# A feed-forward by seven block products: another sequence of the products, second buffers for two block sums, and other places for the first activation slabs

## The chip, the cores and the metric

One core of a Trainium2 chip runs one launch that computes two transformer blocks on a sequence of 1024 tokens. The metric is the device time of that core in microseconds (us). Three timed runs of the kernel before took 2768.13, 2770.41 and 2771.04 us, so the median is 2770.41 us.

## The reference, cut to what matters

Everything is float32. The change touches only the feed-forward of the first block and the hand-over into it and out of it. `conv_glu_ffn` multiplies the normed input h (1024 tokens x 1024 features) with `ffn_w_up` (1024 x 5632), runs a causal depthwise convolution of three taps with a bias over tokens, multiplies silu(gate) by value, and multiplies the product (1024 x 2816) with `ffn_w_down`:

```python
x = x + conv_glu_ffn(rmsnorm(x, ffn_norm_g[l]), ffn_w_up[l], ffn_conv_w[l],
                     ffn_conv_b[l], ffn_w_down[l])
```

## The kernel before, in words

**Numbers.** Every float32 matrix product is made of three products of rounded parts (`dot3`, L980): high weight by high activation, high by low, low by high. A high part is a rounding copy, on ScalarE for the weights of this stage (`high_...`, L2079 to L2111) and for activations (`t_high_part`, `b2_high_part`, `block_high`, `diff_high`); a low part is the value less its high part, on GpSimd for the weights (`pair_part`, L882) and on VectorE for activations (`t_low`, `b1_low`, `b2_low`).

**Up product.** The 5632 output features are 22 pairs (one gate tile and one value tile of 128 features). A pair is a 2 x 2 block product: the weights' blocks are A11, A12 (gate; first and second half of the contraction) and A21, A22 (value); the activations' blocks are B11, B21 (tokens 0 to 511) and B12, B22 (tokens 512 to 1023). Seven block products of twelve matmuls each (four 128-slices of contraction, three parts) replace eight, with the block sums S1 = A21+A22, S2 = S1-A11, S3 = A21-A11, S4 = A12-S2 made by GpSimd for every pair, and T1, T2, T3, T4 of the activations made once by VectorE (`t_diff`). The products, in the order before, are A11 B11, S1 T1, S3 T3, S2 T2, A12 B21, S4 B22, A22 T4. They go into four half banks a, c, d, b of `gemm0` and `gemm1`; A12 B21 is added onto a, S4 B22 onto c, A22 T4 onto d, and a copy of what stood there must be out first: `snapshot(p, 0)` of a, `snapshot(p, 1)` of c (ScalarE, L2162), and VectorE's sum of d with that copy of c (L2978). VectorE's further sums (`up_sums`, `up_gate`, `up_value`) give gate and value, scaled per token by WIDE_FF; then come the convolution taps (ScalarE `tap2` for the last, VectorE `tap` for the others), Silu (ScalarE `gate`), their product (VectorE `product`), and its store to `act_spill` in HBM.

**Where things lie.** h_hi/h_lo hold B11 and T1 in slices 0 to 3, B21 and B22 in slices 4 to 7. T2, T3, T4 have buffers of their own. S2, S3 and S4 have one buffer each, so GpSimd waits for the product of the pair before (`prod_mm`) that read them.

**Entry.** The norm's factor of a token (1/rms) is not applied to h; the sums of squares (`add_square`, VectorE) go through 16 thin matmuls (`token_sums`, L1138), a root (ScalarE, L2160), a reciprocal (VectorE, L2968), a spread over partitions (`spread`, L1144, before product 7 of pair 0) and a copy into WIDE_FF (ScalarE, L2223). Each is queued at one place of its engine's written order. The last tile of the residual x (m = 7) is added by VectorE at L2938, after the last matmul of the layer before.

**Down product.** Eleven steps per half of the output features, each of 48 matmuls, read `act_spill` back in slabs of two tiles. The slabs go through a ring of three buffers, those of T3, T2 and T4 (`RING`, `ring_load`, `ring_high_part`, `ring_low`). A step waits for its split weights (`w_split`; GpSimd, `split_slot`) and for both low halves of its slab (`ring_ready`); step 0 also for VectorE's last reads of the banks.

**What sets the order.** Nothing is planned at run time: each engine's instructions are written out in one order (SP's for loads and stores), each waits on counting semaphores, and an engine stands still at the first wait that is not met.

Of the kernel before, what the change touches and what calls it, by code (L numbers as in the profile page):

```python
# [8 lines left out]
F32 = mybir.dt.float32  # L9
F32R = mybir.dt.float32r  # L10
I32 = mybir.dt.int32
ALU = mybir.AluOpType
# [109 lines left out]
RING = [(i, i % N_RING) for i in range(FF_STEPS)] + [(i, N_RING - 1 - i % N_RING) for i in range(FF_STEPS - 2)]  # L122
# [71 lines left out]
def build(nc, w_stream, x_t, mem_t, positions, vecs, rows, small_w, pool_w, consts, x_spill, c_rows, out):  # L194
    ctx = ExitStack()
    with ctx:
# [31 lines left out]
        hhi = sb("h_hi", [P, KT, S], F32R)  # L228
        hlo = sb("h_lo", [P, KT, S], F32R)
        with nc.sbuf_tensor("pair_ex_f", [P, KT, P], F32) as pair_ex_f, nc.sbuf_tensor("v_gate1_r", [P, KT, P], F32R) as v_gate1_r, \  # L230
                nc.sbuf_tensor("v_val1_r", [P, KT, P], F32R) as v_val1_r:
            pass
        with nc.sbuf_tensor("pair_ex", [P, KT, P], F32R) as pair_ex, nc.sbuf_tensor("v_gate1", [P, KT, P], F32) as v_gate1, \
                nc.sbuf_tensor("v_val1", [P, KT, P], F32) as v_val1, nc.sbuf_tensor("taps", [P, 4, S], F32) as taps:
# [36 lines left out]
        S2_V, S3_V, S4_V = pair_ex_f[:, LO, :], wlo_f0[:, LO, :], wlo_f1[:, LO, :]  # L271
        S2_R, S3_R, S4_R = pair_ex[:, LO, :], wlo[0][:, LO, :], wlo[1][:, LO, :]
# [8 lines left out]
        def lows(p):  # L281

            gate, val = r_pair[p % 2]
            return gate[:, LO, :], val[:, LO, :], S3_R, S2_R, gate[:, HI, :], S4_R, val[:, HI, :]
# [5 lines left out]
        ring_f = [flat4(t3_lo_f), flat4(t2_lo_f), flat4(t4_lo_f)]  # L290
        X = xres[:, :, :].rearrange("p k s -> p (k s)")
# [59 lines left out]
        T_ORDER = [(k, n) for k in range(2) for n in range(3)] + [(2, 0), (2, 1), (3, 0), (3, 1), (2, 2), (3, 2)]  # L351

        def t_at(k, n):

            return T_ORDER.index((k, n)) + 1
# [263 lines left out]
        def _(sp):  # L619
# [66 lines left out]
            ring_load(0)  # L686
            act_store(PAIRS - 2)
            ring_load(1)
            down_load(2)
            ring_load(2)  # L690
            down_load(3)
            act_store(PAIRS - 1)
            for e in range(4, len(DOWN)):
                if e == 4:
# [3040 lines left out]
```

## Time and profile before

| | us |
|---|---|
| median of three timed runs | 2770.41 |
| the profiled execution | 2770.92 |
| its span, first to last instruction | 2769.1 |
| PE busy in the span | 2711.5 |
| DVE, POOL, ACT busy in the span | 1433.2, 1121.4, 1051.2 |

PE is TensorE, DVE is VectorE, ACT is ScalarE, POOL is GpSimd, SP is the engine that issues most transfers. A time stamp is in us from the span's start. The up product of pair 0 begins at about 672 us, the down product at about 1121 us. A matmul's listed duration overlaps the next one's; the distance of two starts tells the pace. "Idle before" is the time an engine stood still ahead of an instruction, with what released it.

### The profile page before, as it was taken

The numbers are of one execution on the slowest core, as the hardware profiler recorded it, in microseconds if no ns is written. First come the engines' busy times: TensorE is split into PE (matmuls) and PEld (weight loads), VectorE is DVE, ScalarE is ACT, GpSimd is POOL, SyncE is SP. The second block draws the span as 40 slices with busy tenths as digits, with TensorE's granted clock in tenths as the row PEclk, the third lists the DMA queues.
The fourth block names the chain that finished last, engine by engine and source line by source line (L and its number), as shares of the span: only waits on it lengthen the run. The fifth ranks groups of instructions, "written<-read, shape, count | busy, mean of one in ns | idle before, by whom it ended". The sixth has DMA issues, their size and how long they took to land.

```text
span 2769.1 us, 34511 instructions
## 1 busy us (share of the span) xinstructions
PE 2711.5 (98%) x13574; PEld 2190.9 (79%) x13574; DVE 1433.2 (52%) x2014; ACT 1051.2 (38%) x1598; POOL 1121.4 (40%) x625
## 2 busy tenths in 40 slices
PE   8999999998999999999999999999998999999998
PEld 6888787777788888788878888888876777777776
DVE  7344643137656666422456666666545444444455
ACT  5322222334444444221245455454434333333342
POOL 4333453224676767434322222222345333333335
PEclk9999999999999999999999999999998999999999
DMA  4012231002122222554322222222222111111114
GB/s 152 31 46 74 102 100 53 31 28 102 69 83 77 85 76 84 198 175 138 114 87 72 56 64 72 64 71 64 57 99 86 41 39 38 38 38 39 38 52 163
DMA packets 111785, 214.21 MB, mean 77 GB/s; under 512 B 32032, under 2 KB 61888, under 8 KB 111504
## 3 DMA queue, kind: packets, MB, share of 16 engines
q1 hardware_dynamic: 104992, 190.02, 20.9%
q10 hardware_dynamic: 6192, 20.18, 2.0%
q8 instruction: 108, 1.77, 0.3%
q0 software_dynamic: 448, 1.88, 0.2%
q14 instruction: 45, 0.37, 0.0%
HBM read 177.38 MB, written 34.67 MB: 77 GB/s over the span
## 4 chain that ended last, share of the span: by engine, by line
PE 90%; DVE 5%; ACT 2%; issue 2%; DMA 1%; POOL 0%; SPq 0%; ACTq 0%; DVEq 0%; POOLq 0%
PE gemm L982 21%; PE gemm L983 21%; PE gemm L984 21%; PE small L1164 2%; PE small L1702 2%; PE small L1680 2%; PE small L984 1%; PE small L983 1%; PE small L982 1%; PE small L1690 1%; PE small L1552 1%; PE gemm L1105 1%; PE gemm L1109 1%; PE gemm L1108 1%; PE small L1277 1%
## 5 line engine op out<-in xcount | busy, mean ns | idle before, releaser
L982 PE MATMUL gemm<-h_hi,w_hi 128*128 128x512 f32 x2120 | 902.1, 426 | 21.5 <-DVE h_lo L2674 8.9
L983 PE MATMUL gemm<-h_lo,w_hi 128*128 128x512 f32 x2120 | 840.4, 396 | 0.0
L984 PE MATMUL gemm<-h_hi,w_lo 128*128 128x512 f32 x1944 | 769.7, 396 | 0.0
L796 POOL TENSOR_TENSOR w_hi<-w_raw,unit_col 128x1024 fp32r<-128x1024 f32 x134 | 264.4, 1973 | 1133.9 <-PE gemm L984 888.8
L982 PEld LDWEIGHTS gemm<-h_hi,w_hi 128*128 128x128 f32 x2120 | 401.6, 189 | 108.5 <-issue 13.3
L983 PEld LDWEIGHTS gemm<-h_lo,w_hi 128*128 128x128 f32 x2120 | 402.2, 190 | 79.3 <-issue 6.2
L984 PEld LDWEIGHTS gemm<-h_hi,w_lo 128*128 128x128 f32 x1944 | 366.3, 188 | 88.7
L805 POOL TENSOR_TENSOR w_lo<-w_raw,w_hi 128x1024 fp32r<-128x1024 f32 x118 | 305.6, 2590 | 13.8 <-DVE w_lo L2833 4.9
L943 POOL TENSOR_TENSOR w_hi<-w_raw,unit_col 128x1024 fp32r<-128x1024 f32 x32 | 60.7, 1896 | 324.6 <-PE gemm L984 324.6
L2503 ACT ACTIVATE xres<-xres,stat 128x128 f32<-128x128 f32 (+3 forms) x64 | 49.7, 777 | 206.0 <-DVE stat L3508 205.2
L3030 DVE TENSOR_TENSOR t_lo<-t_lo_f,t_hi 128x1024 fp32r<-128x1024 f32 x40 | 48.9, 1264 | 149.3 <-ACT t_hi L2205 149.3
L3012 DVE SCALAR_TENSOR_TENSOR small<-norm,vec,small 128x1024 f32<-128x1024 f32 x84 | 108.1, 1287 | 30.7 <-ACT small L2191 28.4
L3502 DVE SCALAR_TENSOR_TENSOR xres<-small,rstd_cols,xres 128x128 f32<-128x128 f32 x64 | 22.5, 351 | 175.0 <-PE small L1680 166.5
L982 PE MATMUL gemm<-t_hi,w_hi 128*128 128x512 f32 x264 | 105.3, 399 | 0.6 <-DVE norm L2993 0.3
L983 PE MATMUL gemm<-t_lo,w_hi 128*128 128x512 f32 x264 | 105.0, 398 | 0.0
L984 PE MATMUL gemm<-t_hi,w_lo 128*128 128x512 f32 x264 | 104.3, 395 | 0.0
L2205 ACT ACTIVATE t_hi<-t_lo_f 128x1024 fp32r<-128x1024 f32 x40 | 40.2, 1051 | 161.2 <-DMA t_lo_f<-act_spill 161.2
L2587 ACT ACTIVATE xres<-small 128x512 f32<-128x512 f32 (+2 forms) x96 | 47.1, 490 | 106.1 <-PE small L1690 105.4
L2191 ACT ACTIVATE small<-norm,vec 128x1024 f32<-128x1024 f32 x42 | 50.7, 1207 | 75.9 <-DVE norm L2993 74.1
L1702 PEld LDWEIGHTS small<-xres 128*128 128x128 f32 x576 | 74.1, 191 | 5.7
L945 POOL TENSOR_TENSOR w_lo<-w_raw,w_hi 128x1024 fp32r<-128x1024 f32 x32 | 76.5, 2392 | 2.5
L1702 PE MATMUL small<-xres 128*128 128x128 f32 x576 | 74.5, 274 | 0.0
(526 smaller groups left out, 5176.9 us busy)
## 6 DMA issues: line engine op xcount, KB each, us to landing
w_raw<-w_stream SPq DMA_DIRECT2D x178, 512.0 KB, 3.5
t_lo_f<-act_spill SPq DMA_DIRECT2D x40, 512.0 KB, 4.3
act_spill<-taps SPq DMA_DIRECT2D x22, 512.0 KB, 2.7
x_spill<-xres ACTq DMA_DIRECT2D x16, 512.0 KB, 2.6
v_gate<-w_stream SPq DMA_DIRECT2D x11, 512.0 KB, 3.4
v_val<-w_stream SPq DMA_DIRECT2D x11, 512.0 KB, 3.4
xres<-x_t SPq DMA_DIRECT2D x8, 512.0 KB, 8.6
xres<-x_t ACTq DMA_DIRECT2D x8, 512.0 KB, 5.1
```

What stands on the lines that cost most here:

```text
L796: nc.gpsimd.tensor_tensor(whi[d][:, :, :], raw[s][:, :, :], unit, ALU.mult).then_inc(w_hi_done, 1)
L805: nc.gpsimd.tensor_tensor(wlo[d][:, :, :], raw[s][:, :, :], whi[d][:, :, :].bitcast(F32), ALU.subtract).then_inc(w_split, 1)
L943: nc.gpsimd.tensor_tensor(whi[s][:, :, :], raw[s][:, :, :], unit, ALU.mult).then_inc(w_hi_done, 1)
L945: nc.gpsimd.tensor_tensor(wlo[s][:, :, :], raw[s][:, :, :], whi[s][:, :, :].bitcast(F32), ALU.subtract).then_inc(w_split, 1)
L982: mm(dst, w_hi, a_hi, start=first, stop=False, skip_group_check=onto)
L983: mm(dst, w_hi, a_lo, start=False, stop=False, skip_group_check=onto)
L984: return mm(dst, w_lo, a_hi, start=False, stop=last, skip_group_check=onto)
L1164: last = nc.tensor.transpose(ck(dst, n), ck(src, n), ident)
L1680: last = mm(pa[:, c:c + w], ck(yt[:, g, :], q), H[:, g % 2, c:c + w], start=True, stop=True)
L1702: last = mm(ck(pb, 4 + q % 4), ck(X4(0), b), ck(X4(5), b), start=(b == 0), stop=(b == q))
L2191: A(tap_sum(p, v), Nf[:, v * FP + 2:v * FP + 2 + S], ACT.Identity, bias=vc("ff_b", q), scale=vc("ff_w", 2 * 2 * PAIRS + q)).then_inc(ff_ta ...
L3012: ins = V.scalar_tensor_tensor(c, Nf[:, v * FP + n:v * FP + n + S], vc("ff_w", 2 * PAIRS * n + q), c, ALU.mult, ALU.add)
```

## The change: what it does

- The products come in the sequence A11 B11, S1 T1, A12 B21, S4 B22, S3 T3, S2 T2, A22 T4, for all pairs. The waits, GpSimd's low parts, ScalarE's high parts and VectorE's sums are put into an order to match.
- S2 and S3 get a second buffer (`sum_ex`), used by odd pairs. GpSimd now waits for the products of the pair but one before; for S4 it waits as before.
- Between the product that `snapshot` copies and the one that is added onto it there is now one other product; before there were three.
- In pair 0, VectorE and ScalarE make the parts of B21 and B22 ahead of most of T2 to T4; the token sums stand after product 5, not 4; the spread stays ahead of product 7.
- In each pair `tap2(p - 1, 1)` is moved ahead of `snapshot(p, 0)`; `u2_copy` comes after the high parts of S1, A12, S4 and S3 of the next pair; VectorE's sums are regrouped (`up_gate`, `up_gate_late`, `up_value`).
- The first two slabs of the down product go to two new ring slots in h_hi/h_lo slices 0 to 3, loaded as soon as product 2 of the last pair is done. In the last pair VectorE makes the low parts of slab 0 after `up_gate_late`, and those of slab 1 after `up_value`.

The core of the diff:

```diff
-RING = [(i, i % N_RING) for i in range(FF_STEPS)] + [(i, N_RING - 1 - i % N_RING) for i in range(FF_STEPS - 2)]
+RING = [(0, N_RING), (1, N_RING + 1)] + [(i, (i - 2) % N_RING) for i in range(2, FF_STEPS)] + \
+       [(i, (0, 2, 1)[i % N_RING]) for i in range(FF_STEPS - 2)]
...
-        S2_V, S3_V, S4_V = pair_ex_f[:, LO, :], wlo_f0[:, LO, :], wlo_f1[:, LO, :]
-        S2_R, S3_R, S4_R = pair_ex[:, LO, :], wlo[0][:, LO, :], wlo[1][:, LO, :]
+        S2_V, S3_V, S4_V = (pair_ex_f[:, LO, :], sum_ex_f[:, LO, :]), (wlo_f0[:, LO, :], sum_ex_f[:, HI, :]), wlo_f1[:, LO, :]
+        S2_R, S3_R, S4_R = (pair_ex[:, LO, :], sum_ex[:, LO, :]), (wlo[0][:, LO, :], sum_ex[:, HI, :]), wlo[1][:, LO, :]
...
+        for k in (0, 2):
+            ring_hi.append(hhi[:, k:k + 2, :])
+            ring_lo.append(hlo[:, k:k + 2, :])
+            ring_f.append(hlo_f[:, k:k + 2, :])
...
-                if j < N_RING:
-                    sp.wait_ge(*prod_mm(PRODUCTS * (PAIRS - 1) + (3, 4, 7)[j]))
+                if j < N_RING + 2:
+                    sp.wait_ge(*prod_mm(PRODUCTS * (PAIRS - 1) + (2, 2, 5, 6, 7)[j]))
...
-                pair_part(p, 2, S3_V, W_S3, highs + 2)
+                pair_part(p, 1, a21, W_S1, highs + 2)
                 if p:
-                    pool.wait_ge(*prod_mm(done_mm + 6))
+                    pool.wait_ge(*prod_mm(PRODUCTS * (p - 1) + 4))
                 else:
                     pool.wait_ge(pe_slot, T_FF)
-                nc.gpsimd.tensor_tensor(S4_V, a12, S2_V, ALU.subtract).then_inc(pair_sum.sem, 1)
+                nc.gpsimd.tensor_tensor(S4_V, a12, s2, ALU.subtract).then_inc(pair_sum.sem, 1)
                 pool.wait_ge(*pair_sum(sums_at + 4))
-                pair_part(p, 3, S2_V, W_S2, highs + 4)
-                pair_part(p, 4, a12, W_A12, highs + 5)
-                pair_part(p, 5, S4_V, W_S4, highs + 6)
+                pair_part(p, 2, a12, W_A12, highs + 3)
+                pair_part(p, 3, S4_V, W_S4, highs + 4)
+                pair_part(p, 4, s3, W_S3, highs + 5)
+                pair_part(p, 5, s2, W_S2, highs + 6)
                 pair_part(p, 6, a22, W_A22, highs + 7)
...
-                low, high = lows(p)[j], (W_A11, W_S1, W_S3, W_S2, W_A12, W_S4, W_A22)[j]
+                low, high = lows(p)[j], (W_A11, W_S1, W_A12, W_S4, W_S3, W_S2, W_A22)[j]
...
+                bank, onto = UP_BANKS[(0, 2, 0, 2, 3, 1, 3)[j]], j in (2, 3, 6)
                 pe.wait_ge(*pair_split(PRODUCTS * p + j + 1))
-                if p == 0 and j in (0, 2):
-                    pe.wait_ge(tile_added, 2 * KT - 1 + j // 2)
+                if p == 0 and j in (0, 4):
+                    pe.wait_ge(tile_added, 2 * KT - 1 + j // 4)
                 if p and j == 0:
-                    pe.wait_ge(*ff_out(3 * p))
-                if p and j in (1, 2):
-                    pe.wait_ge(*ff_scaled(2 * (p - 1) + j))
-                if j in (4, 5):
-                    pe.wait_ge(*snap(3 * p + j - 3))
+                    pe.wait_ge(*ff_out(3 * p - 2))
+                if p and j in (1, 4, 5):
+                    pe.wait_ge(*ff_scaled(2 * p - 1 if j == 1 else 2 * p))
+                if j in (2, 3):
+                    pe.wait_ge(*snap(3 * p + j - 1))
                 if j == 6:
-                    pe.wait_ge(*ff_out(3 * p + 1))
+                    pe.wait_ge(*ff_out(3 * p + 2))
...
-                    if p == 0 and j == 3:
+                    if p == 0 and j == 4:
                         pe.wait_ge(sq_added, KT * (NFF + 1))
                         token_sums(pa[:, 0:NB], N[:, 2, :]).then_inc(norm_mm, 1)
...
-                        if k == 1:
-                            gained_block(2)
                     high_s1(0)
-                    high_s3(0)
-                    for n in range(2):
-                        t_high_part(2, n)
-                    for k in range(4, KT - 1):
-                        b2_high_part(k)
+                    b2_high_part(4)
+                    b2_high_part(5)
+                    gained_block(2)
+                    b2_high_part(6)
                     square(NFF, m, xres[:, m, :])
+            b2_high_part(KT - 1)
+            gained_block(3)
+            high_a12(0)
+            high_s4(0)
+            square(NFF, KT - 1, xres[:, KT - 1, :])
+            high_s3(0)
+            t_high_part(2, 0)
             t_high_part(3, 0)
-            t_high_part(3, 1)
             high_s2(0)
-            square(NFF, KT - 1, xres[:, KT - 1, :])
-            b2_high_part(KT - 1)
-            high_a12(0)
-            t_high_part(2, 2)
-            t_high_part(3, 2)
-            high_s4(0)
-            high_a22(0)
...
+            def highs_between(p):
+
+                high_s1(p)
+                high_a12(p)
+                high_s4(p)
+                high_s3(p)
+
             for p in range(PAIRS):
                 more = p + 1 < PAIRS
+                if p:
+                    tap2(p - 1, 1)
                 snapshot(p, 0)
+                if p == 0:
+                    high_a22(0)
                 if more:
                     high_a11(p + 1)
                 if p:
-                    tap2(p - 1, 1)
                     gate(p - 1)
                 snapshot(p, 1)
                 if p == 0:
+                    t_high_part(2, 1)
+                    t_high_part(3, 1)
+                    t_high_part(2, 2)
+                    t_high_part(3, 2)
                     mean_root()
-                    high_s3(1)
-                    high_s1(1)
-                    high_s2(1)
-                    u2_copy(0)
                     act.wait_ge(norm_wide, W_FF + 1)
                     A(WIDE_FF, pa, ACT.Copy).then_inc(wide_out, 1)
-                if p and more:
-                    high_s3(p + 1)
-                    high_s1(p + 1)
-                    high_s2(p + 1)
-                if p:
-                    u2_copy(p)
                 if more:
-                    high_a12(p + 1)
+                    highs_between(p + 1)
                 else:
                     ring_high_part(0)
+                u2_copy(p)
+                if more:
+                    high_s2(p + 1)
+                else:
+                    ring_high_part(1)
                 tap2(p, 0)
                 if more:
-                    high_s4(p + 1)
                     high_a22(p + 1)
-                else:
-                    ring_high_part(1)
...
-                        t_diff(2, n)
-                    for n in range(2):
-                        t_low(2, n)
+                    b2_low(4)
+                    b2_low(5)
+                    t_diff(2, 0)
                 if m in (4, 5):
                     for n in range(3):
                         t_diff(m - 4, n)
@@ -2953,40 +2975,42 @@
                         t_low(m - 4, n)
                 if m < KT - 2:
                     add_square(NFF, m)
-            for n in range(3):
-                t_diff(3, n)
+            b2_low(6)
+            b2_low(7)
+            t_diff(2, 1)
+            t_diff(3, 0)
+            t_diff(3, 1)
+            t_low(2, 0)
             t_low(3, 0)
-            b2_low(4)
-            t_low(3, 1)
-            for k in range(5, KT):
-                b2_low(k)
             add_square(NFF, KT - 2)
             add_square(NFF, KT - 1)
-            t_low(2, 2)
-            t_low(3, 2)
+            t_diff(2, 2)
+            t_diff(3, 2)
+            for n in (1, 2):
+                t_low(2, n)
+                t_low(3, n)
...
+            def up_gate(p):
                 a, b, c, d = UP_BANKS
                 dve.wait_ge(*prod_mm(PRODUCTS * p + 3))
-                dve.wait_ge(*snap(3 * p + 2))
-                V.tensor_tensor(SNAP5, d, SNAP5, ALU.add).then_inc(ff_out.sem, 1)
-                dve.wait_ge(*prod_mm(PRODUCTS * p + 4))
-                V.tensor_tensor(b, b, SNAP1, ALU.add).then_inc(ff_out.sem, 1)
-            def up_gate(p):
-                a, b, c, d = UP_BANKS
-                dve.wait_ge(*prod_mm(PRODUCTS * p + 5))
                 if p == 0:
                     dve.wait_ge(wide_out, 2)
                 V.tensor_tensor(Nf[:, 2:2 + HALF], a, WIDE_FF[:, half(0)], ALU.mult).then_inc(ff_out.sem, 1)
+                dve.wait_ge(*prod_mm(PRODUCTS * p + 5))
+                dve.wait_ge(*snap(3 * p + 2))
+                V.tensor_tensor(SNAP5, d, SNAP5, ALU.add).then_inc(ff_out.sem, 1)
                 dve.wait_ge(*prod_mm(PRODUCTS * p + 6))
+                V.tensor_tensor(b, b, SNAP1, ALU.add).then_inc(ff_out.sem, 1)
+            def up_gate_late(p):
+                a, b, c, d = UP_BANKS
                 dve.wait_ge(*snap(3 * p + 3))
                 done(V.tensor_tensor(c, c, U2, ALU.add))
...
             for p in range(PAIRS):
-                up_sums(p)
+                up_gate(p)
+                up_gate_late(p)
                 if p == PAIRS - 1:
                     ring_low(0)
-                up_gate(p)
-                if p == PAIRS - 1:
-                    up_value(p)
-                tap(p, 0, 1)
-                if p < PAIRS - 1:
-                    up_value(p)
-                tap(p, 0, 0)
+                up_value(p)
                 if p == PAIRS - 1:
                     ring_low(1)
+                tap(p, 0, 1)
+                tap(p, 0, 0)
                 tap(p, 1, 1)
                 tap(p, 1, 0)
```

## Rows read from the trace of the kernel before

**Rows 1.** The page: the engines, and the chain that ended last.
```profile
PE 2711.5 (98%) x13574; PEld 2190.9 (79%) x13574; DVE 1433.2 (52%) x2014; ACT 1051.2 (38%) x1598; POOL 1121.4 (40%) x625
PE 90%; DVE 5%; ACT 2%; issue 2%; DMA 1%; POOL 0%; SPq 0%; ACTq 0%; DVEq 0%; POOLq 0%
```

**Rows 2.** Waits of PE, 640 to 1330 us: in total, times, longest.
```profile
PE small L1138 <- DVE norm L2630: 6.2, 1, 6.2
PE gemm L982 <- DVE t_lo L2919: 2.0, 1, 2.0
```

**Rows 3.** Stretches: length, then busy PE, PEld, DVE, ACT, POOL, granted clock, DMA.
```profile
700.00:702.00 2.00, 2.00 (x6) 1.52 (x6) 0.16 (x1) 0.80 (x2) 2.00 (x2) 0.50 0.00 0
704.00:706.00 2.00, 2.00 (x9) 1.60 (x8) 0.00 (x0) 0.00 (x0) 0.00 (x0) 0.90 0.51 145
780.00:1100.00 320.00, 320.00 (x1377) 257.96 (x1376) 195.96 (x212) 145.80 (x212) 231.55 (x182) 1.00 0.23 82
```

**Rows 4.** Timeline, PE: start, length, line and operation, idle before.
```profile
433.64 1.84 PE L1138 MATMUL small<-const,head 128*128 128x1 f32 x16
435.34 0.48 PE L982 MATMUL gemm<-h_hi,w_hi 128*128 128x512 f32 x1
...
678.53 0.47 PE L982 MATMUL gemm<-t_hi,w_lo 128*128 128x512 f32 x1 [1.23 <-issue]
...
694.82 3.58 PE L1138 MATMUL small<-const,norm 128*128 128x1 f32 x16 [6.25 <-DVE norm L2630]
698.26 0.77 PE L982 MATMUL gemm<-h_hi,w_hi 128*128 128x512 f32 x1
...
706.72 1.04 PE L1144 MATMUL small<-const,rstd_cols 128*128 128x128 f32 x8
707.51 0.48 PE L982 MATMUL gemm<-t_hi,pair_ex 128*128 128x512 f32 x1
...
730.11 0.39 PE L982 MATMUL gemm<-h_hi,w_hi 128*128 128x512 f32 x1
```

**Rows 5.** Timeline, DVE, ACT and POOL, at the entry.
```profile
666.82 0.75 DVE L2927 SCALAR_TENSOR_TENSOR h_lo<-norm,vec,h_hi 128x512 fp32r<-128x512 f32 x1
667.48 1.80 DVE L2924 SCALAR_TENSOR_TENSOR h_lo<-xres,vec,h_hi 128x512 fp32r<-128x512 f32 x1
...
677.22 1.21 DVE L2938 TENSOR_TENSOR xres<-gemm,xres 128x1024 f32<-128x1024 f32 x1
...
683.41 1.14 ACT L2077 ACTIVATE h_hi<-xres,vec 128x1024 fp32r<-128x1024 f32 x1
684.45 0.61 ACT L2101 ACTIVATE w_hi<-w_raw 128x512 fp32r<-128x512 f32 x1
...
707.79 1.03 ACT L2223 ACTIVATE norm<-small 128x1024 f32<-128x1024 f32 x1 [6.99 <-PE small L1144]
...
667.41 1.32 POOL L907 TENSOR_TENSOR pair_ex_f<-w_raw 128x512 f32<-128x512 f32 x1 [4.05 <-DMA x_keep<-xres]
```

**Rows 6.** Timeline, DVE and ACT, pair 10, which starts at 886.46.
```profile
904.18 0.69 DVE L2993 TENSOR_TENSOR norm<-gemm,norm 128x512 f32<-128x512 f32 x1
904.91 1.21 ACT L2191 ACTIVATE small<-norm,vec 128x1024 f32<-128x1024 f32 x1 [3.62 <-DVE norm L2993]
908.67 1.23 DVE L3003 TENSOR_TENSOR norm<-gemm,norm 128x1024 f32<-128x1024 f32 x1
```

**Rows 7.** Timeline, DVE, POOL and PE, where the down product begins.
```profile
1117.02 2.36 DVE L3030 TENSOR_TENSOR t_lo<-t_lo_f,t_hi 128x1024 fp32r<-128x1024 f32 x2 [3.47 <-ACT t_hi L2205]
1132.68 4.05 DVE L3030 TENSOR_TENSOR t_lo<-t_lo_f,t_hi 128x1024 fp32r<-128x1024 f32 x2
...
1118.49 2.65 POOL L796 TENSOR_TENSOR w_hi<-w_raw,unit_col 128x1024 fp32r<-128x1024 f32 x1 [4.00 <-PE gemm L984]
1121.21 2.41 POOL L805 TENSOR_TENSOR w_lo<-w_raw,w_hi 128x1024 fp32r<-128x1024 f32 x1
...
1121.46 0.47 PE L982 MATMUL gemm<-t_hi,w_hi 128*128 128x512 f32 x1 [0.34 <-DVE norm L2993]
```

More of the change, by code:

```diff
@@ L349, in build, with t_made, t_rounded @@
         T1_F = Nf[:, 0:KT // 2 * HALF].rearrange("p (k s) -> p k s", s=HALF)
-        T_ORDER = [(k, n) for k in range(2) for n in range(3)] + [(2, 0), (2, 1), (3, 0), (3, 1), (2, 2), (3, 2)]
-        def t_at(k, n):
-            return T_ORDER.index((k, n)) + 1
+        T_FIRST = [(k, n) for k in range(2) for n in range(3)]
+        SUM_ORDER = T_FIRST + [(2, 0), (2, 1), (3, 0), (3, 1), (2, 2), (3, 2)]
+        HIGH_ORDER = T_FIRST + [(2, 0), (3, 0), (2, 1), (3, 1), (2, 2), (3, 2)]
+        def t_made(k, n):
+            return t_sum(SUM_ORDER.index((k, n)) + 1)
+        def t_rounded(k, n):
+            return t_high(HIGH_ORDER.index((k, n)) + 1)
         def tap_sum(p, v):
@@ L686, in _ @@
             ring_load(0)
+            ring_load(1)
             act_store(PAIRS - 2)
[L688 to L691, printed above, removed]
+            for j in range(2, 5):
+                ring_load(j)
+            for e in (2, 3):
+                down_load(e)
             act_store(PAIRS - 1)
             for e in range(4, len(DOWN)):
-                if e == 4:
-                    ring_load(3)
-                elif e < 13:
+                if 6 <= e < 13:
                     ring_load(e - 1)
@@ L888, in _ @@
                 a11, a12, a21, a22 = values(p)
-                done_mm, highs, sums_at = PRODUCTS * (p - 1), PRODUCTS * p, 4 * p
+                s2, s3 = S2_V[p % 2], S3_V[p % 2]
+                highs, sums_at = PRODUCTS * p, 4 * p
                 for v in range(2):
                     pool.wait_ge(*pair_in[p % 2][v](16 * (p // 2 + 1)))
-                if p:
-                    pool.wait_ge(*prod_mm(done_mm + 3))
-                else:
-                    pool.wait_ge(pe_slot, T_FF - 1)
-                nc.gpsimd.tensor_tensor(S3_V, a21, a11, ALU.subtract).then_inc(pair_sum.sem, 1)
+                if p == 0:
+                    pool.wait_ge(pe_slot, T_FF - 1)
+                elif p == 1:
+                    pool.wait_ge(x_kept, 16 * KT)
+                    pool.wait_ge(*b2_ready(KT // 2))
+                    pool.wait_ge(*t_made(3, 2))
+                    pool.wait_ge(sq_ready, KT * (NFF + 1))
+                else:
+                    pool.wait_ge(*prod_mm(PRODUCTS * (p - 2) + 5))
+                nc.gpsimd.tensor_tensor(s3, a21, a11, ALU.subtract).then_inc(pair_sum.sem, 1)
                 pool.wait_ge(*pair_sum(sums_at + 1))
@@ L1372, in up_product @@
                     last = dot3(bank, high[:, k, :], low[:, k, :], x_hi[:, k, :], x_lo[:, k, :],
-                                k == 0 and j < 4, k == KT // 2 - 1, j >= 4)
+                                k == 0 and not onto, k == KT // 2 - 1, onto)
                 last.then_inc(prod_mm.sem, 1)
@@ L2169, in u2_copy @@
             def u2_copy(p):
-                act.wait_ge(*ff_out(3 * p + 2))
+                act.wait_ge(*ff_out(3 * p + 3))
                 if p:
```

77 lines of the change are left out of this document (39 added, 38 removed).

## The prediction

> **What bounds the kernel now.** I read the page first: PE is busy for 2711.5 of 2769.1 us and makes up 90% of the chain that ended last [rows 1]. So only time in which PE stands, or runs at the lower of its two clocks (1.2 GHz, granted 0.5, against 2.4 GHz), can change the end. The stretches then say where that is: from 780 to 1100 us, some 16 of the 22 pairs, PE is busy for all of 320.00 us at a granted clock of 1.00, with 1377 matmuls, so one each 0.233 us [rows 3]. A product is 12 x 0.233 = 2.8 us, a pair 19.55 us. The change adds and drops no matmul, so pairs 2 to 20 can't gain. What is left is the entry (pairs 0 and 1) and the start of the down product. The waits of PE show the entry: 6.2, 2.0 and, as the timeline has it, 1.23 us [rows 2, 4]. After the 6.25 us gap the clock is granted at 0.50 until about 704.4 [rows 3], while the products run from 698.26. At the down product PE waits 0.34 us [rows 7].
>
> Pair 0 starts at 671.9, product 2 ends at about 677.5 and pair 2 starts at 730.11 [rows 4]. I rebuild that stretch in the new order, each engine taking its instructions in turn, and do the same for one inner pair and for the last.
>
> **VectorE and GpSimd against each other.** A VectorE operation with two SBUF operands took 0.75 us alone, and 1.80 us when GpSimd had begun one of 1.32 us 0.07 us before it [rows 5]. Two of ring_low took 2.36 us alone and 4.05 us while GpSimd was splitting a weight tile; where VectorE was first, GpSimd's took 2.65 us [rows 7]. I read this as turns: who comes second waits for the other's whole instruction.
>
> **Entry, up to product 3.** VectorE now has B1's low parts, two of B2 and one T difference before the last residual tile: it adds that at 675.6 instead of 677.22 [rows 5] (estimate, in turns with GpSimd). From its end at 676.85, ScalarE does, one start after the other: b2 high 1.05 us, gained block 0.6, A12 0.5, S4 0.5, square 0.95, S3 0.5, T 0.55, and is at 681.6 (distances of starts; whole instructions are 1.14 and 0.61 us [rows 5]). Its next, the high part of T3's slice 3, needs VectorE's third operation in a queue of b2_low, b2_low (1.25 us each), t_diff, t_diff: these two fall on GpSimd's low parts of A12 and S4, in turns 1.7 us each, so 682.8. Then 0.55 for T, 0.55 for S2, 0.6 for `snapshot(0, 0)`: 684.5. Product 3 is added onto a and waits for it. PE thus stands from 677.5 to 684.5, 7.0 us in one piece.
>
> **The clock.** After 6.25 us of standing PE ran products at 0.50 from 698.26 to about 704.4, 6.2 us [rows 3, 4]. A matmul then takes about twice 0.233 less its fixed part, 0.43 us. I take 6.2 us here too: of the 24 matmuls of products 3 and 4, 14.5 run at 0.43 us, the rest at 0.233: 8.5 us instead of 5.6, to 693.0. The ends are half of that time (product 4 done at 691.5) and twice of it (695.5).
>
> **Rest of pair 0.** Product 5, 2.8: 695.8. Token sums: 16 take 1.70 us to the next start at full clock, against 3.44 before [rows 4]: 697.5. Product 6: 700.3. Its T2 parts are covered: VectorE's low parts in turns with GpSimd's first sums of pair 1 end at 695.2 (slice 3 of T2) and 698.6 (T4), the reciprocal at 698.8, so the spread (0.79 us before a product [rows 4]) needs no wait. It ends at 701.2, against 707.5 before: 6.3 us won. Call this point X.
>
> **What is late next.** Product 7 now needs d's sum, which stands in VectorE's order behind a x WIDE_FF, which needs ScalarE's copy of the spread: start at X+0.28, 1.03 us [rows 4, 5], then 0.7 and 0.65: product 7 starts at X+2.75. Behind the copy, ScalarE also holds the highs of pair 1 ahead of `u2_copy`: S1 (X+1.8); GpSimd S1 low and S4 sum, 1.3 each (X+4.5); high S4, high S3, `u2_copy` (X+6.2); VectorE c+U2, c x WIDE (X+7.7), then value (X+10.15); ScalarE tap2 1.2, `snapshot(1, 0)` 0.6: X+11.95. Product 3 of pair 1, ready to run at X+11.1, waits for it, then Silu's table (1.3 us) and `gate(0)` hold `snapshot(1, 1)` to X+15.4, 0.6 us too late for product 4. Product 4 and three more follow: pair 2 starts at X+26.6 = 727.8, against 730.11. **Entry: 2.3 us won**, of 6.3. Bounds: X 1.4 us earlier is where VectorE's reciprocal binds (3.7 won); X 2.8 us later with the longer clock (0.5 lost).
>
> **Inner pairs.** Time from a pair's first matmul. VectorE's c x WIDE (0.69 us) ends at 19.8, the last product at 19.55; two sums of 0.6 and 0.7 later value is scaled (1.23 us), to 22.35; tap2 (1.21 us) ends at 23.6 [rows 6], `snapshot(p+1, 0)` at 24.1; product 3 wants it at 25.15: 1.05 us to spare. `gate(p)` ends at 25.95, `snapshot(p+1, 1)` at 26.45, wanted at 27.95. GpSimd's S4 sum goes from 11.55, when product 4 frees its buffer; A22's low part ends at 22.9, wanted at 36.3. The weights' value tile is loaded at 0.2 as before; the queued act_store goes behind it as before. So nothing: cost 0, covered by 1.05 us; were the cover gone by 0.5 us, it would cost 0.5 a pair. The moved tap2 has no one behind it but the snapshot.
>
> **The start of the down product.** In the last pair b+SNAP1 ends at 17.7, `u2_copy` at 18.35, c+U2 19.1, c x WIDE 19.8, and only then comes ring_low(0), which step 0 waits for. Before, ring_low(0) was done at 1119.38 [rows 7], inside the pair. Alone it is 2.36 us: 22.2. But GpSimd, released by product 5 at 14.35, splits tile T_FF until 18.7 and begins T_FF+1's high part (1.9 us) at 18.8, ahead of ring_low. In turns: that to 20.75, ring_low's first to 21.9, GpSimd's low part (2.3) to 24.2, the second to 25.35. PE, done at 19.55, starts at 25.4: 5.9 us idle, against 0.49 before: **5.4 us lost**; alone it would be 2.2. The next wait (value scaled, 27.9) is behind step 0's first quarter, 28.2. The early slabs themselves gain nothing: from 1140 us on there was no wait on the ring.
>
> The clock again: of products at 0.5, (0.43-0.233)/0.43 = 0.45 of the time is lost. After 6.25 us of standing these were 6.2 us [rows 3, 4], a loss of 2.8. The gap here is a little shorter; as an estimate I take 5 us at 0.5: **2.2 us lost**. The ends are 0 and 5.6.
>
> The Trainium skill's page "SBUF — State Buffer", section "Who interferes with whom", says that a VectorE instruction with two SBUF inputs contends with a GpSimd one that reads SBUF, and the second fully blocks. By that rule ring_low(0) is done at 25.35; if they shared the port at no price it would be 22.2 and the sum 2 us. The trace agrees, with 4.05 us for two that take 2.36 alone [rows 7]; of all rules it speaks most against this change.
>
> **Sum.** -2.3 + 5.4 + 2.2 = +5.3 us on the profiled execution's 2770.92: 2776.2. That run lies 0.5 us above the median of 2770.41; as a median I say 2776.
>
> **Rivals.**
> - Nothing measurable: the two don't meet on the port (GpSimd's split is a little later), the idle time is 2.7 us and the clock stays: +2.2; with the entry's -2.3 it is 0, 2770.5; with half the clock's price +1.5. For it: a shift of 1 us of GpSimd's start decides. Against: GpSimd had no wait in that place but the product's. 0.2.
> - Faster: the entry keeps what it wins. If neither d's sum nor `u2_copy` nor the snapshots make PE wait, pair 2 starts 22.3 us behind X and the entry is worth 6.6; with X at its early bound 8.0. With a down product that loses 2.2 that is -5.8: 2764.6. It decides if the chain behind WIDE_FF's copy brings `u2_copy`'s sum in under 5.6 us instead of 7.7. Rows 4 and 5 speak against it. 0.1.
> - Slower still: an inner snapshot is late by more than its 1.05 us, at 0.3 us over in 20 pairs +6, or the half clock lasts twice as long in both places: 2781 to 2783. For it: two snapshots that had three products of time now have one. 0.2.
> - That the second buffers free GpSimd and shorten each pair: excluded by 320.00 of 320.00 us.
>
> **How the numbers follow.** About 0.2% (5.5 us) is what a measurement of this kernel can tell from no change. The forecast has 0.5, 2773.5 to 2778.5 its own range, and lies across that bound: 0.27 above, 0.23 within. With the rivals: slower 0.27+0.2 = 0.47, same 0.23+0.2 = 0.43, faster 0.1. The range is 2767 to 2783.
>
> **What would show it.** PE idle 7 us after product 2 of pair 0, released by ScalarE's copy of a; half clock after it; the spread at 701 and pair 2 at 728; waits of about 1 us in pair 1 on the copies; 320 of 320 us inside; PE idle 5 to 6 us before the down product, released by t_lo L3030's counterpart, with the pair of GpSimd and VectorE interleaved. I am wrong if the idle time at the down product is under 3 us, if X comes before 699, or if an inner pair takes over 19.6 us.

## The result, and the profile after

The changed kernel took 2772.32 us in the median of 20 runs, the kernel before 2769.38 us in 20 runs beside them: ratio 1.0014, 95% interval 1.0007 to 1.0020. It is a little slower, and by less than the 0.2% that the prediction took as its bound. The forecast was 5.3 us slower on the profiled execution, 2776 us as a median. Measured in medians it is 2.9 us, about half of that: 2772.32 us lies inside the whole range (2767 to 2783) and 1.2 us below the forecast's own range (2773.5 to 2778.5). The profiled execution of the changed kernel has a span of 2770.5 us, 1.4 more than before.

The page first: its engines and its chain are nearly those of [rows 1]. PE is busy 1.4 us less, though the span is 1.4 us longer: the kernel stands more and works at half clock less.

```profile
PE 2710.1 (98%) x13574; PEld 2190.9 (79%) x13574; DVE 1437.5 (52%) x2014; ACT 1052.3 (38%) x1598; POOL 1122.4 (41%) x625
PE 91%; DVE 4%; issue 2%; ACT 2%; POOL 1%; DMA 0%; ACTq 0%; SPq 0%; DVEq 0%; POOLq 0%
```

PE's waits of the changed kernel, 640 to 1330 us (what waits, releaser: total, times, longest), beside [rows 2]: 14.8 us now, in five places; before it was 10.0 us, also in five. "issue" is the wait ahead of product 7 of pair 0.

```profile
PE gemm L1003 <- POOL w_lo L900: 6.2, 1, 6.2
PE gemm L1003 <- DVE h_lo L3054: 5.2, 1, 5.2
PE gemm L1003 <- issue: 2.6, 1, 2.6
PE gemm L1003 <- ACT poolw L2184: 0.5, 1, 0.5
PE gemm L1003 <- ACT tiny L2184: 0.3, 1, 0.3
```

PE's timeline of the changed kernel, beside [rows 4] and the last row of [rows 7]: product 3, the token sums, the spread, product 7, then products 3 and 4 of pair 1, pair 2, and the down product.

```profile
683.49 0.77 PE L1003 MATMUL gemm<-h_hi,w_hi 128*128 128x512 f32 x1 [6.21 <-POOL w_lo L900]
693.74 1.84 PE L1159 MATMUL small<-const,norm 128*128 128x1 f32 x16
698.32 1.03 PE L1165 MATMUL small<-const,rstd_cols 128*128 128x128 f32 x8
701.91 0.47 PE L1003 MATMUL gemm<-t_hi,pair_ex 128*128 128x512 f32 x1 [2.55 <-issue]
...
711.03 0.47 PE L1003 MATMUL gemm<-h_hi,w_hi 128*128 128x512 f32 x1 [0.50 <-ACT poolw L2184]
714.37 0.47 PE L1003 MATMUL gemm<-h_hi,w_lo 128*128 128x512 f32 x1 [0.31 <-ACT tiny L2184]
725.59 0.39 PE L1003 MATMUL gemm<-h_hi,w_hi 128*128 128x512 f32 x1
...
1122.25 0.77 PE L1003 MATMUL gemm<-h_hi,w_hi 128*128 128x512 f32 x1 [5.23 <-DVE h_lo L3054]
```

Pair 2 begins at 725.59 instead of 730.11. The stretches of the changed kernel, with the columns of [rows 3]: the clock is at 0.50 at 682 and back by 688; all of the 320 us inside is busy; and it is at 0.50 again after the wait at the down product.

```profile
682.00:684.00 2.00, 0.51 (x1) 0.50 (x2) 2.00 (x2) 2.00 (x5) 2.00 (x2) 0.50 0.90 324
686.00:688.00 2.00, 2.00 (x7) 1.55 (x7) 1.92 (x2) 0.00 (x0) 1.94 (x2) 0.65 0.00 0
...
780.00:1100.00 320.00, 320.00 (x1376) 257.89 (x1375) 197.53 (x215) 147.90 (x212) 229.71 (x180) 1.00 0.24 81
...
1122.00:1124.00 2.00, 1.75 (x4) 1.50 (x5) 1.97 (x4) 0.00 (x0) 0.00 (x0) 0.50 0.92 305
1126.00:1128.00 2.00, 2.00 (x6) 1.58 (x6) 2.00 (x2) 0.00 (x0) 0.00 (x0) 0.57 0.00 0
1128.00:1130.00 2.00, 2.00 (x10) 1.59 (x10) 1.96 (x3) 0.57 (x1) 0.00 (x0) 1.00 0.00 0
```

Where the down product begins, VectorE, GpSimd and ScalarE of the changed kernel, beside [rows 7]:

```profile
1117.01 5.13 DVE L3054 TENSOR_TENSOR h_lo<-h_lo_f,h_hi 128x1024 fp32r<-128x1024 f32 x2
...
1115.90 1.88 POOL L811 TENSOR_TENSOR w_hi<-w_raw,unit_col 128x1024 fp32r<-128x1024 f32 x1
1117.86 3.20 POOL L820 TENSOR_TENSOR w_lo<-w_raw,w_hi 128x1024 fp32r<-128x1024 f32 x1
...
1107.90 2.01 ACT L2222 ACTIVATE h_hi<-h_lo_f 128x1024 fp32r<-128x1024 f32 x2 [3.77 <-DMA h_lo_f<-act_spill]
```

Read it in turns. GpSimd's high part ends at 1117.78, in ring_low's first 0.8 us; then ring_low's first operation, 1.1 us; then GpSimd's low part, to 1121.06; then ring_low's second, to 1122.14; PE at 1122.25. The slab had been there, with its high parts, since 1109.9.

PE issues the same number of matmuls in both kernels, so the n-th of one can be set against the n-th of the other. Shift in us against the first profile of before (minus is earlier); two kernels were profiled twice:

| | pair 2 | down product begins | its step 0 done | end of the span |
|---|---|---|---|---|
| before, again | -1.4 | -1.4 | -1.4 | 0.0 |
| after | -4.5 | +0.8 | +3.3 | +1.4 |
| after, again | -5.6 | -0.3 | +2.3 | +2.5 |

The code of the stages behind the down product is the same, and yet the changed kernel's delay shrank there by 1.9 us in one execution and not in the other, and before, again, lost the 1.4 us that it had won. So single profiles are good to some 1.5 us at the end, and I compare the terms at their place. The mean of the two profiles of after, less that of the two of before, is -4.4 us at pair 2, +3.5 at the end of step 0 and +2.0 at the end of the span.

### The profile page after: what moved, and what is told of

The parts are those of the page before. It is cut to its first block, busy times and chain, and to the rows that moved or that the text cites. A ratio compares the mean times of both kernels' runs of the same rounds, so it can differ in the third digit from the quotient of the medians.

```text
span 2770.5 us, 34512 instructions
## 1 busy us (share of the span) xinstructions
PE 2710.1 (98%) x13574; PEld 2190.9 (79%) x13574; DVE 1437.5 (52%) x2014; ACT 1052.3 (38%) x1598; POOL 1122.4 (41%) x625
## 4 chain that ended last, share of the span: by engine, by line
PE 91%; DVE 4%; issue 2%; ACT 2%; POOL 1%; DMA 0%; ACTq 0%; SPq 0%; DVEq 0%; POOLq 0%
PE gemm L1003 21%; PE gemm L1004 21%; PE gemm L1005 21%; PE small L1185 2%; PE small L1723 2%; PE small L1701 2%; PE small L1003 1%; PE small L1004 1%; PE small L1005 1%; PE small L1711 1%; PE small L1573 1%; PE gemm L1126 1%; PE small L1298 1%; PE small L1318 1%; PE small L1560 1%
## 5 line engine op out<-in xcount | busy, mean ns | idle before, releaser
L1003 PE MATMUL gemm<-t_hi,w_hi 128*128 128x512 f32 x248 | 98.2, 396 | 0.0
L1004 PE MATMUL gemm<-t_lo,w_hi 128*128 128x512 f32 x248 | 98.2, 396 | 0.0
L1005 PE MATMUL gemm<-t_hi,w_lo 128*128 128x512 f32 x204 | 80.6, 395 | 0.0
L1701 PE MATMUL small<-head,yt 128*128 128x512 f32 (+2 forms) x192 | 72.4, 486 | 0.0
```

The lines of the kernel that those rows point to most:

```text
L1003: mm(dst, w_hi, a_hi, start=first, stop=False, skip_group_check=onto)
L1004: mm(dst, w_hi, a_lo, start=False, stop=False, skip_group_check=onto)
L1005: return mm(dst, w_lo, a_hi, start=False, stop=last, skip_group_check=onto)
L1701: last = mm(pa[:, c:c + w], ck(yt[:, g, :], q), H[:, g % 2, c:c + w], start=True, stop=True)
```

## The experiments

All are edits of the changed kernel; each was timed beside the kernel before on the same chip, and the ratio is to that.

**1. The low parts of slab 0 earlier**

```diff
                 V.tensor_tensor(Nf[:, 2:2 + HALF], a, WIDE_FF[:, half(0)], ALU.mult).then_inc(ff_out.sem, 1)
+                if p == PAIRS - 1:
+                    ring_low(0)
                 dve.wait_ge(*prod_mm(PRODUCTS * p + 5))
...
                 up_gate_late(p)
-                if p == PAIRS - 1:
-                    ring_low(0)
                 up_value(p)
```

> Edit: in the last pair VectorE makes the low parts of slab 0 behind the scaling of a (where it stands idle for 4.5 us) and not behind up_gate_late. Theory (the queue place of ring_low is the whole loss at the down product): PE's gap of 5.23 us there falls to 0.3 to 0.5 us, no stretch at granted clock 0.5 follows, so 5.0 + 2.4 = 7.4 us less than the changed kernel up to 1150 us; of such a shift 1 to 2 us can be lost again in the stages behind, as 1.9 us of the changed kernel's delay was regained there. As a median 2765 to 2768 where the kernel before has 2769.4. Rival (the early slabs or their transfers are late, or the banks are not read out in time): the gap stays above 2 us.

Measured: 2765.80 us, ratio 0.9990 (0.9981 to 0.9999). VectorE, PE and a stretch of this kernel:

```profile
1108.51 2.36 DVE L3056 TENSOR_TENSOR h_lo<-h_lo_f,h_hi 128x1024 fp32r<-128x1024 f32 x2 [2.21 <-ACT h_hi L2222]
...
1116.59 0.48 PE L1003 MATMUL gemm<-h_hi,w_hi 128*128 128x512 f32 x1 [0.23 <-DVE norm L3019]
```
```profile
1120.00:1130.00 10.00, 10.00 (x45) 8.02 (x44) 9.86 (x9) 5.83 (x7) 1.80 (x1) 1.00 0.46 185
```

The low parts take 2.36 us in a place where GpSimd does nothing, PE waits 0.23 us, and the clock stays at 1.00. Pair 2 stood at -5.2, the end of step 0 at -4.9 (of the table's shifts). The wait and its half clock, 7.4 us in the changed kernel, are gone, and nothing came in their place. This shows the two large terms of the loss, and that the slower end was not forced by the sequence of the products.

**2. GpSimd held back**

```diff
             pool.wait_ge(*prod_mm(PRODUCTS * (PAIRS - 1) + 6))
+            pool.wait_ge(*ring_ready(2))
             split_slot(T_FF + 1, 1, T_FF // 2 + 1)
```

> Edit: GpSimd begins the split of the second down tile only when both low parts of slab 0 are done; ring_low stays where it is. Theory (turns on the shared port): the two ring_low operations take 2.4 us instead of 5.13, PE's gap falls from 5.23 to 2.5 us; the clock may stay at full, then 2.7 + 2.4 = 5.1 us less than the changed kernel, else 2.7. Rival (ring_low is slow for another reason, such as the 1.5 MB of transfers landing then): it still takes about 5 us.

Measured: 2767.45 us, ratio 0.9996 (0.9987 to 1.0005). VectorE, PE and GpSimd of this kernel, and a stretch:

```profile
1117.94 2.35 DVE L3055 TENSOR_TENSOR h_lo<-h_lo_f,h_hi 128x1024 fp32r<-128x1024 f32 x2
1120.39 0.47 PE L1004 MATMUL gemm<-h_hi,w_hi 128*128 128x512 f32 x1 [2.46 <-DVE h_lo L3055]
1120.43 1.90 POOL L811 TENSOR_TENSOR w_hi<-w_raw,unit_col 128x1024 fp32r<-128x1024 f32 x1 [3.57 <-issue]
```
```profile
1120.00:1130.00 10.00, 9.61 (x41) 7.79 (x42) 9.93 (x9) 1.67 (x2) 4.30 (x2) 1.00 0.57 206
```

One wait on the other engine, with ring_low left where it was, takes its pair of operations from 5.13 to 2.35 us. So 2.8 of the 5.2 us were the two engines' turns, the other 2.4 the place of ring_low in the order. After the wait of 2.46 us the clock stayed at 1.00, where 5.23 us were followed by 0.50 in both executions of the changed kernel. This is one execution, and the same one had 0.50 after its gap of 2.55 us before product 7; that the shorter wait always keeps the clock here is not shown.

**3. The copy of a first, in the entry**

```diff
             high_s4(0)
+            snapshot(0, 0)
             square(NFF, KT - 1, xres[:, KT - 1, :])
```

(At its old place it is left out for pair 0.)

> Edit: ScalarE makes snapshot(0, 0) right behind the high part of S4, ahead of five other operations. Theory: product 3 of pair 0 starts with A12's low part at 681.3 us instead of 683.5 (gap 4.0 instead of 6.2). Then the next wait takes over, the reciprocal of the norm behind VectorE's four T low parts at 696.3, so the spread comes at 696.5 instead of 698.3 and pair 2 starts 1.8 us earlier. If the clock stays low longer after the shorter gap, product 5 starts late and it is 0 to 1. Rival (everything behind is bound by VectorE's queue alone): 0.

Measured: 2770.60 us, ratio 1.0003 (0.9994 to 1.0013). PE of this kernel, product 3 and the spread:

```profile
681.08 0.79 PE L1003 MATMUL gemm<-h_hi,w_hi 128*128 128x512 f32 x1 [3.97 <-POOL raw_r L900]
696.28 1.09 PE L1165 MATMUL small<-const,rstd_cols 128*128 128x128 f32 x8 [0.49 <-DVE rstd_cols L2994]
```

Only a copy on ScalarE was moved, and PE's wait fell from 6.21 to 3.97 us. So the copy was the releaser, though the wait's row names GpSimd's `w_lo`. The next thing late is the reciprocal, as the prediction's early bound had it, but at 696.28 instead of 698.8, so that it cost only 0.49 us. Of the 2.4 us, pair 2 kept 1.7 (-6.2 against -4.5), and only 0.6 against the changed kernel's second profile (-5.6). Here the wait of 2.55 us before product 7 was followed by a stretch of 0.50 from 701.4 to 704.8, which the changed kernel did not have; by the prediction's 0.45 it cost 1.5 us.

**4. The ring of before under the new sequence**

```diff
-RING = [(0, N_RING), (1, N_RING + 1)] + ...
+RING = [(i, i % N_RING) for i in range(FF_STEPS)] + [(i, N_RING - 1 - i % N_RING) for i in range(FF_STEPS - 2)]
...
+                if j < N_RING:
+                    sp.wait_ge(*prod_mm(PRODUCTS * (PAIRS - 1) + (5, 6, 7)[j]))
...
                 up_value(p)
                 if p == PAIRS - 1:
-                    ring_low(1)
+                    ring_low(0)
                 tap(p, 0, 1)
                 tap(p, 0, 0)
+                if p == PAIRS - 1:
+                    ring_low(1)
```

(SP's order of loads, the places of ScalarE's high parts and one count go back with it.)

> Edit: the new product sequence with the ring of three buffers of before; slab 0 is loaded when product 5 of the last pair has freed T3's buffer, its high parts stand behind u2_copy, its low parts behind the value. Theory A (the early slots are what lets the new sequence reach the down product at all): slab 0 lands about 5.5 us after product 5, at 19.7 us of the pair, its low parts are done at 23 to 25, PE's gap is 3.5 to 5.5 us; so about as slow as the changed kernel, and against e1_low_early 4 to 7 us slower. Theory B (the early slots gain nothing): PE's gap is under 1 us.

Measured: 2773.52 us, ratio 1.0016 (1.0007 to 1.0025). ScalarE, VectorE and PE of this kernel:

```profile
1118.46 2.00 ACT L2222 ACTIVATE t_hi<-t_lo_f 128x1024 fp32r<-128x1024 f32 x2 [0.80 <-DMA t_lo_f<-act_spill]
1121.55 2.91 DVE L3054 TENSOR_TENSOR t_lo<-t_lo_f,t_hi 128x1024 fp32r<-128x1024 f32 x2
1124.56 0.77 PE L1003 MATMUL gemm<-t_hi,w_hi 128*128 128x512 f32 x1 [5.52 <-DVE t_lo L3054]
```

T3's buffer, free before after product 3, is now read until product 5, and the slab comes when the pair is nearly over. The wait is 5.52 us: no shorter than with the early slabs. The early slabs gain next to nothing as the change uses them (0.3 us of wait), and 7.7 us in medians once ring_low stands early (2773.52 against 2765.80, same chip).

**5. Pair 0: the sums of b and d before the scaling of a**

```diff
                 V.tensor_tensor(b, b, SNAP1, ALU.add).then_inc(ff_out.sem, 1)
+                if p == 0:
+                    dve.wait_ge(wide_out, 2)
+                    V.tensor_tensor(Nf[:, 2:2 + HALF], a, WIDE_FF[:, half(0)], ALU.mult).then_inc(ff_out.sem, 1)
```

(The same operation is left out ahead of them in pair 0, and three counts are adapted.)

> Edit: in pair 0 VectorE makes d's and b's sums before it scales a with WIDE_FF, so product 7 does not wait for WIDE_FF. Theory (two chains of equal length behind the copy of WIDE_FF): PE's gap of 2.55 us ahead of product 7 goes, and the same time is waited in pair 1, for c's scaling (about 1.8 us) and for the two snapshots; pair 2 starts at 725.6 as before, within 0.4 us, and the total does not move (0 to 0.4 us less than the changed kernel). Rival (the gap is on the path by itself): pair 2 starts 2.5 us earlier.

Measured: 2771.11 us, ratio 1.0007 (0.9998 to 1.0016). PE of this kernel:

```profile
708.59 0.47 PE L1003 MATMUL gemm<-h_hi,w_hi 128*128 128x512 f32 x1 [1.89 <-DVE norm L3019]
```

Product 7 had no wait any more: its 2.55 us were the wait for d's sum behind the copy of the spread. The chain behind that copy then let PE wait 1.89 us in pair 1. Pair 2 stood at -2.7; this profile was already 1.3 us late ahead of pair 0, so net -4.1, no better than the changed kernel's -4.5. But the 1.89 us were followed by a stretch of 0.50 from 710.1 to 713.5, about 1.5 us by the 0.45. So part of what the edit won went there, and not to the next link of the chain.

**6. The same, with `u2_copy(0)` ahead of pair 1's high parts**

```diff
+                if p == 0:
+                    u2_copy(p)
                 if more:
                     highs_between(p + 1)
```

> Edit: as e4_sums_first, and ScalarE copies U2 of pair 0 right behind WIDE_FF, ahead of pair 1's high parts. Theory: c is scaled at about 702.5 instead of 706.7 and no longer late; the wait that is left is for snapshot(1, 0), which stands behind tap2(0, 1), about 1.7 us, and for snapshot(1, 1), 0.6 us; pair 2 starts at 724.1, 1.5 us earlier than in the changed kernel. Rival: 0, because tap2 is bound by GpSimd's S4 sum for pair 1.

Measured: 2770.63 us, ratio 1.0005 (0.9996 to 1.0014). PE of this kernel:

```profile
709.49 0.47 PE L1003 MATMUL gemm<-h_hi,w_hi 128*128 128x512 f32 x1 [1.44 <-POOL sum_ex_r L900]
712.84 0.47 PE L1003 MATMUL gemm<-h_hi,w_lo 128*128 128x512 f32 x1 [0.32 <-ACT tiny L2184]
```

The order is right (scaling, `u2_copy`, taps, copy), and the next link still binds: the copy of a in pair 1 behind `tap2`. Pair 2 stands at -6.1, 1.6 us better than the first profile of the changed kernel and 0.4 better than the second: by itself this gain is no larger than the difference of two executions.

**7. All together, and the copies of pair 1 ahead of the taps**

Experiments 1, 3 and 6, and:

```diff
+                if p == 1:
+                    snapshot(p, 0)
                 if p:
                     tap2(p - 1, 1)
-                snapshot(p, 0)
+                if p > 1:
+                    snapshot(p, 0)
...
+                if p == 1:
+                    snapshot(p, 1)
                 if p:
                     gate(p - 1)
-                snapshot(p, 1)
+                if p != 1:
+                    snapshot(p, 1)
```

(In pair 0, `tap2(0, 0)` also goes ahead of the high part of S4 of pair 1.)

> Edit: e1_low_early, e3_snap_first and e5_sums_u2 together, and for pair 1 the two snapshots ahead of tap2(0, 1) and gate(0), tap2(0, 0) ahead of the high part of S4. Theory (the terms add): 7.4 at the down product, 1.8 at product 3, 3 at pair 1: 12 us less than the changed kernel up to 1150 us, pair 2 at 720 to 721; behind it 1 to 3 us may be lost again. As a median 2760 to 2764, 6 to 9 under the kernel before.

Measured: 2758.79 us, ratio 0.9969 (0.9957 to 0.9981). It is the fastest of all, 10 us under the kernel before, and 1.2 us under the range that was expected. PE's waits, 640 to 1330 us, in full:

```profile
PE gemm L1003 <- POOL raw_r L900: 4.0, 1, 4.0
PE gemm L1003 <- DVE norm L3037: 0.2, 1, 0.2
```

No wait is left in pairs 0 and 1 but the one before product 3. Pair 2 stands at -10.4 and the end of step 0 at -10.1. On a third chip:

> The best version once more. Expected 2757.5 to 2760 us, 9 to 11 under the kernel before; its profile again without a stretch at granted clock 0.5 at the down product.

Measured: 2759.74 us, ratio 0.9964 (0.9951 to 0.9978); -10.4 and -10.2 at the two places. That is inside the expected 2757.5 to 2760, but 8.5 us under the kernel before in medians, not 9 to 11.

**8. The two kernels once more**

> The changed kernel itself on the same chip, to have it beside the others. Expected: 2.5 to 3.5 us over the kernel before, its profile with the gaps of 6.2, 2.6 and 5.2 us.

Measured: 2772.24 us, ratio 1.0010 (1.0001 to 1.0019). The gaps of 2.55 and 5.23 us came again, the first one not: it was 4.62 us. PE at product 3, and VectorE's last residual add, in this profile:

```profile
682.60 0.48 PE L1003 MATMUL gemm<-h_hi,w_hi 128*128 128x512 f32 x1 [4.62 <-POOL w_lo L900]
674.76 1.21 DVE L2961 TENSOR_TENSOR xres<-gemm,xres 128x1024 f32<-128x1024 f32 x1
```

The add came 0.9 us earlier than in the first profile (675.66), and ScalarE's operations up to the copy of a with it. VectorE and GpSimd had met at other moments. One VectorE operation, in the first profile and in this one:

```profile
667.78 1.78 DVE L2950 SCALAR_TENSOR_TENSOR h_lo<-norm,vec,h_hi 128x512 fp32r<-128x512 f32 x1
667.92 0.74 DVE L2950 SCALAR_TENSOR_TENSOR h_lo<-norm,vec,h_hi 128x512 fp32r<-128x512 f32 x1
```

In the first, GpSimd had begun an operation at 667.45, here only at 668.13. PE paid 0.7 us of it back, as product 2 ended that much later (0.30 us of it is a wait for GpSimd's low part before product 1). Why GpSimd began later is not shown.

> The kernel before once more, for a second profile of it. Open is whether the 2.1 us by which its first profile waits more than every later one between 1490 and 1680 us (1.4 us for VectorE L3359, 0.7 us for L3320) belong to this kernel or to that one execution. If to the kernel, they stand here too and the changed kernel regains 2 us behind the feed-forward; if to the execution, they are gone or another size and the changed kernel's true cost is near the 3.3 us that it has at 1150 us. As a median within 1 us of the kernel before.

Measured: 2768.21 us, ratio 0.9999 (0.9990 to 1.0008). PE's waits, 1385 to 1700 us, of the first profile of before and then of this one:

```profile
PE small L1474 <- DVE state L3359: 1.4, 1, 1.4
PE small L1552 <- DVE xres L3320: 0.7, 1, 0.7
```
```profile
PE small L1552 <- DVE xres L3320: 0.7, 1, 0.7
```

The wait of 1.4 us, which neither profile of the changed kernel has and which seemed to be won behind the change, belongs to one execution of the kernel before, not to its code. The clock differs too, by executions of the same kernel. PE's sums of this profile start as in [rows 4] (694.82, after 6.25 us), and 702 to 704 us reads:

```profile
694.76 3.58 PE L1138 MATMUL small<-const,norm 128*128 128x1 f32 x16 [6.19 <-DVE norm L2630]
```
```profile
702.00:704.00 2.00, 2.00 (x11) 1.59 (x10) 0.00 (x0) 0.00 (x0) 0.29 (x1) 1.00 0.21 23
```

In the first profile the stretches on both sides of it are at 0.50 and 0.90 [rows 3], and that one is at 0.50:

```profile
702.00:704.00 2.00, 2.00 (x7) 1.52 (x6) 0.00 (x0) 0.00 (x0) 0.32 (x1) 0.50 0.00 0
```

The lower clock lasted 3.4 us longer there, about 1.5 us by the 0.45. That is the 1.4 us at pair 2 in the table.

## Why the prediction was right, point by point

The terms on the profiles, in us (the terms are differences of the table's columns):

| term | forecast | after | after, again |
|---|---|---|---|
| entry, up to pair 2 | -2.3 | -4.5 | -5.6 |
| wait at the down product, with the inner pairs | +5.4 | +5.3 | +5.3 |
| its half clock | +2.2 | +2.5 | +2.6 |
| sum at the end of step 0 | +5.3 | +3.3 | +2.3 |

Against the second profile of before the sums are +4.7 and +3.7, all of the difference in the entry (-3.1 and -4.2). Whichever pair of profiles is taken, the entry won more than foretold and the down product lost what was foretold. With the means of two profiles each, the entry is -4.4 and the sum +3.5. So the direction and the two mechanisms were right, and the size was forecast too large, mainly because the entry's gain was put too low; 3.5 is near the 2.9 and 3.4 us of the two pairs of medians.

- **Up to product 3: right, 1 us off.** The last residual add came at 675.66 (675.6 foretold), product 3 at 683.49 (684.5): T3's slice 3 was ready about 1 us before the time reckoned, as VectorE began the first of the two differences just ahead of GpSimd's operation and had no turn to wait for (0.75 us, reckoned 1.7). The releaser was the copy of a; experiment 3 showed it, the name in the row would not have.
- **The clock at the entry: the mis-sized term.** I took all of 6.2 us of products at half clock from [rows 3, 4]. In the changed kernel 0.50 began while PE still stood, and products ran at it for about 3.9 us, to 687.4. These are 2.3 us less at half clock, by the prediction's 0.45 a cost 1.0 us smaller. With the 1.0 us of product 3, the spread's end (X) came at 699.1 instead of 701.2. And the row itself was one execution's: before, again, had 0.50 for 3.4 us less. In the second profile of after X was 698.0. The prediction called itself wrong if X came before 699: by that sign its entry was wrong in this execution, and right by 0.1 us in the first. (Its late end for product 4, 695.5, should be 694.8, as 24 x 0.43 is 10.3 us, with another 1.0 us falling into product 5; its 2.8 us for X is right.)
- **From there on: right.** Counted from X, in the first profile: product 7 at 2.80 us (2.75), product 3 of pair 1 at 11.92 (11.95), product 4 at 15.26 (15.4), pair 2 at 26.5 (26.6); the second profile has 26.5 too. The entry's gain of 4.5 is the forecast's 2.3 and these 2.1.
- **The faster rival** needed d's sum and `u2_copy` to cost nothing. In the kernel as it is they cost what the prediction had reckoned. Experiments 5 to 7 took them away one after the other; each time the next link took over, until in experiment 7 none was left. There pair 2 stood 5.8 us earlier than in the first profile of the changed kernel, 4.7 than in the second, experiment 3's share included.
- **Inner pairs: right.** 320.00 of 320.00 us. A pair took 19.563 us from product to product, against 19.543: 0.4 us over 20 pairs, which I had at 0; the two profiles of each kernel agree on both. The copies were in time, as foretold. ScalarE, pair 10 of the changed kernel, which starts at 882.10, beside [rows 6]: the copy of a ends 24.1 us into the pair (24.1), the copy of c at 26.4 (26.45).

```profile
904.46 1.21 ACT L2208 ACTIVATE small<-norm,vec 128x1024 f32<-128x1024 f32 x1 [0.77 <-DVE norm L3027]
905.61 0.58 ACT L2184 ACTIVATE poolw<-gemm 128x512 f32<-128x512 f32 x1
...
907.91 0.59 ACT L2184 ACTIVATE tiny<-gemm 128x512 f32<-128x512 f32 x1
```

- **Down product: right**, in size and in mechanism. The row has 5.23 us idle; counted from start to start, as the prediction did, it is 5.4 (5.9), against 0.5 before. So 4.9 of the table's 5.3 are this wait, 0.4 the inner pairs, where I had 5.4 and 0. ring_low took 5.13 us where the turns gave 5.55; experiment 2 showed the turns, experiment 1 the place. The rule of the Trainium skill's page "SBUF — State Buffer", section "Who interferes with whom", is borne out: the second instruction waited for the whole of the first. That is the reading in turns above: 1117.78, 1118.9, 1121.06, 1122.14. The rival of no measurable change, by which the engines would not meet there, is excluded as a mechanism for this kernel; yet the measured change is under 0.2%, the outcome that it named and that had 0.43 in all against 0.47 for slower. It came from the entry, not from the rival's reason. Its +2.2 is near what experiment 2 showed, 2.5 (-3.6 at pair 2, -1.1 at the end of step 0).
- **"The early slabs themselves gain nothing": right only of this kernel.** I argued it from the wait-free ring of before. Experiment 4 showed that under the new sequence the old ring lets PE wait as long, 5.52 us, and beside experiment 1 that the slabs are worth several us. What the slabs bring was held by the place of ring_low.
- **Half clock there: right** by its estimate of 5 us of products at 0.50; they were 5.4, from 1122.25 to about 1127.7.

What stays open: why one pair takes 0.02 us more; why the lower clock lasts longer in one execution than in the next; and where in the unchanged stages behind it an execution wins or loses its 1 to 2 us. None of these turns the result round.

## What to carry to other kernels

A new order that makes data ready earlier is worth only what the operations behind it are moved up by: here the slab was ready 7 us before its low parts were begun, and moving two lines of code took the kernel from 2.9 us above the one before to 2.4 us below it. Where VectorE's two-SBUF-operand operations stand between PE's last matmul and its next, look what GpSimd starts in that moment, and hold it back or put the operation elsewhere. When a wait is removed and the time stays, look for the next link of the same chain: the scaling, `u2_copy` and the two copies of pair 1 came up here one after the other.

## What the runs showed of the hardware that I had not expected

- The stretch at half clock is not a fixed price of a gap. The same kernel had it for 3.4 us longer in one of two executions, after gaps of 6.25 and 6.19 us. A gap of 2.55 us before product 7 was followed by 0.50 in experiments 2, 3 and 4 and not in both executions of the changed kernel nor in experiment 1. A gap of 1.89 us in experiment 5 was followed by 0.50, one of 2.46 us at the down product by 1.00. The gain or loss from a gap is thus known to about 1.5 us only, an estimate from these stretches of 3.4 us and the 0.45.
- Turns repeat. Two VectorE operations of 1.2 us against GpSimd's 1.9 and 2.4 us take 5.13 us, since the second queues again behind GpSimd's next.
- With equal matmuls and no wait, the last product of a pair took 2.77 and 2.73 us (even and odd pairs) before, and 2.77 and 2.75 us after, and a pair 0.02 us more.
